# One order changed in the expert layer: how activations and gates come back from DRAM, which tile is picked first, how many dots stand beside U, and where the lower halves are made

## The reference

```
idx = i1[ci // 16] * 128 + i2[ci % 16];  g = softmax(sc)
act = gelu(sum_d u[idx, d] * h[d]) * g
out = sum_k act[k] * v[idx[k]]          # 8 heads x 16 experts = 128 picks a token
```

## Time and profile before

| what | us |
| --- | --- |
| median of 3 runs | 4067.66 (4053.11 to 4087.13) |
| the profiled execution's own time | 4076.54 |
| its span | 4075.3 |
| TensorE busy in the span | 3770.3 (93%) |
| VectorE busy | 2367.9 (58%) |
| ScalarE busy | 1348.4 (33%) |
| GpSimd busy | 552.5 (14%) |

### The profile page before, as it was taken

One profiled execution on the slowest core, in us unless ns is written; L12 is line 12 of the kernel. 1 busy time (PEld: TensorE's weight loads), 2 busy tenths in 40 slices (PEclk: granted clock), 3 DMA queues, 4 the chain that ended last, 5 costly groups with the idle time before them and its releaser, 6 DMA issues. The chain is left out here.

```text
span 4075.3 us, 46458 instructions
## 1 busy us (share of the span) xinstructions
PE 3770.3 (93%) x18298; PEld 3085.7 (76%) x18298; DVE 2367.9 (58%) x4034; ACT 1348.4 (33%) x2352; POOL 552.5 (14%) x612
## 2 busy tenths in 40 slices
PE   9889999999798999499999788999999999689999
PEld 7767999877776777378787667887888777467877
DVE  5746898877677888743337764332333266933332
ACT  3353333444233333232233334222322233333221
POOL 8500000011444444400000000000000000100000
PEclk9779999999899999799999879999999999789999
DMA  3003465688999999722222102222222221012222
GB/s 125 9 26 94 128 190 178 231 285 285 346 354 344 346 353 343 270 88 93 98 78 74 48 1 73 93 93 98 78 94 96 95 75 55 18 37 83 93 99 73
DMA packets 273433, 574.70 MB, mean 141 GB/s; under 512 B 19952, under 2 KB 159376, under 8 KB 271552
## 3 DMA queue, kind: packets, MB, share of 16 engines
q1 hardware_dynamic: 236256, 437.42, 32.4%
q0 software_dynamic: 36864, 134.23, 9.1%
q10 hardware_dynamic: 96, 0.08, 0.0%
HBM read 517.92 MB, written 53.74 MB: 140 GB/s over the span
## 5 line engine op out<-in xcount | busy, mean ns | idle before, releaser
L348 DVE TENSOR_TENSOR wlast<-wraw,wlast 128x1024 fp32r<-128x1024 f32 x406 | 495.2, 1225 | 506.4 <-ACT wlast L338 505.9
L357 PE MATMUL ps<-XH,wlast 128*128 128x512 f32 (+2 forms) x1888 | 734.0, 389 | 17.4 <-ACT arena L2020 17.4
L359 PE MATMUL ps<-XH,wlast 128*128 128x512 f32 (+2 forms) x1888 | 708.4, 375 | 0.0
L358 PE MATMUL ps<-XL,wlast 128*128 128x512 f32 (+2 forms) x1888 | 707.8, 375 | 0.0
L338 ACT ACTIVATE wlast<-wraw 128x1024 fp32r<-128x1024 f32 x406 | 424.8, 1051 | 246.9 <-PE ps L359 231.6
L348 DVE TENSOR_TENSOR wtwo<-wraw,wtwo 128x1024 fp32r<-128x1024 f32 x212 | 259.4, 1225 | 311.2 <-ACT wtwo L338 310.6
L357 PEld LDWEIGHTS ps<-XH,wlast 128*128 128x128 f32 x1888 | 358.3, 190 | 76.9 <-ACT arena L2020 18.1
L358 PEld LDWEIGHTS ps<-XL,wlast 128*128 128x128 f32 x1888 | 359.1, 190 | 53.5
L359 PEld LDWEIGHTS ps<-XH,wlast 128*128 128x128 f32 x1888 | 357.3, 189 | 55.1
L357 PE MATMUL ps<-XH,wtwo 128*128 128x512 f32 (+1 forms) x960 | 374.5, 390 | 0.0
L358 PE MATMUL ps<-XL,wtwo 128*128 128x512 f32 (+1 forms) x960 | 362.5, 378 | 0.0
(11 more groups left out here) (489 smaller groups left out, 7054.4 us busy)
## 6 DMA issues: line engine op xcount, KB each, us to landing
wraw<-in_ut SPq DMA_DIRECT2D x128, 512.0 KB, 4.1
wraw<-in_v SPq DMA_DIRECT2D x128, 512.0 KB, 7.1
wraw<-in_ffn_gate SPq DMA_DIRECT2D x88, 512.0 KB, 3.5
wraw<-in_ffn_up SPq DMA_DIRECT2D x88, 512.0 KB, 3.5
wraw<-in_ffn_down SPq DMA_DIRECT2D x88, 512.0 KB, 3.4
wraw<-in_w_in SPq DMA_DIRECT2D x58, 512.0 KB, 3.7
acts<-arena SPq DMA_DIRECT2D x128, 192.0 KB, 4.6
gates<-arena SPq DMA_DIRECT2D x12, 2048.0 KB, 10.2
```

Of the source, the lines that this page charges most:

```text
L348: ve.e.tensor_tensor(W.items[n][8], W.rawof(n), W.items[n][7], ALU.subtract).then_inc(*ve.up("wlo", n))
L357: mm(out, lh, rh, start=start, stop=False)
L358: mm(out, lh, rl, start=False, stop=False)
L359: return mm(out, ll, rh, start=False, stop=stop)
```

## The change

- The activations lie in DRAM as 64 pairs (128 partitions x 2 x 384), so that one load brings two turns (384 KB, runs of 3 KB). The stores write half a pair (runs of 1.5 KB). There are three pair buffers instead of six single ones.
- Gates come back for 8 turns at a time (1536 KB, runs of 1 KB) instead of 4 (768 KB, runs of 512 bytes). The DMAs have the same number of runs each.
- At the end of U, SyncE issues two gate loads and three pair loads, one each in items 135 to 139, after that item's weight load and store (`loads0` is 135).
- In the V stage both engines take the weight split and the activation in another order, and the lower half of the activation comes after the dots and rows of the turn.
- The planner orders the units anew: first all that the gathered tile needs, then the other tiles. Its costs and budgets differ a little, and a quota of 1.5 dots an item stands in place of the leftover time. In V, dots and rows are spread at an even pace over 124 turns.
- The arena of that level is larger, since one table (MK) no longer shares memory with the scores.

By the new arithmetic: index known at item 30 (before 44), `norm` at 80 (before 82), gates in items 83 to 130, 90 dots beside U (before 60). Of the 48 gate turns 28 have one dot and 20 have two. Items 131 to 143 have 20 dots, 1 or 2 each, and item 81 has two. V gets 38 dots and 128 rows, one or two a turn (four in two turns), and none is left behind turn 127.

```diff
@@ Peer.__init__
-        ar = k.level(12704)
+        ar = k.level(14752)
...
-        self.ad = k.nc.dram_tensor("acts", (128, 128, TOKENS), F).ap()
+        self.ad = k.nc.dram_tensor("acts", (64, 128, 2 * TOKENS), F).ap()
...
-        self.GC = [ar(4 * DENSE, 4, 32) for _ in range(2)]
-        self.AI = [ar(TOKENS) for _ in range(6)]
+        self.GC = [ar(4 * DENSE, 8, 32) for _ in range(2)]
+        self.AI = [ar(2, TOKENS) for _ in range(3)]
@@ schedule
+        first = [("top", c, GATHERED) for c in range(16)] + [("rows",)] + pick(GATHERED) + [("index",)]
+        tops = [("top", c, i) for c in range(16) for i in range(DENSE)]
+        rest = [u for i in range(DENSE) for u in pick(i)] + [("norm",), ("turned",)]
+        rest += [("gate", n) for n in range(self.GATES)]
...
-            time = min(time, 2.0) + (4.4 if kind == "wq" else 3.0)
+            time = min(time, 1.5) + (4.4 if kind == "wq" else 3.05)
+            quota = min(quota + self.RATE, 2.0) if known is not None and n >= known + 4 else 0.0
             while time > 0:
...
+                late = tops and first and first[0][0] == "top" and tops[0][1] <= first[0][1] - self.SCORES
+                if first and ready(n, first[0]) and not late:
+                    u = first.pop(0)
+                elif tops and ready(n, tops[0]):
+                    u = tops.pop(0)
+                elif not first and not tops and rest and ready(n, rest[0]):
+                    u = rest.pop(0)
+                elif quota >= 1 and dots < PICKS:
+                    u, quota, dots = ("dot", dots), quota - 1, dots + 1
+                else:
                     break
...
+        pace = (len(later) - 4) / 124
         for j in range(128):
-            time = min(time, 1.0) + 1.78
-            while later and time > 0:
+            quota += pace
+            while later and (quota >= 1 or later[0][0] == "act"):
@@ sp_u
+        ahead = [lambda: self.sp_gc(0), lambda: self.sp_back(0), lambda: self.sp_back(1), lambda: self.sp_gc(1),
+                 lambda: self.sp_back(2)]
...
-            if n == self.loads0:
-                for c in range(2):
-                    self.sp_gc(c)
-                for j in range(self.BACK):
-                    self.sp_back(j)
+            if n >= self.loads0 and ahead:
+                ahead.pop(0)()
@@ sp_act
-        sp.e.dma_start(self.ad[j], self.TT[j % 3]).then_inc(...)
+        half = slice(TOKENS * (j % 2), TOKENS * (j % 2) + TOKENS)
+        sp.e.dma_start(self.ad[j // 2, :, half], self.TT[j % 3]).then_inc(...)
@@ sp_gc, sp_back
-            sp.wait_ge(*at("ag", 4 * c - 5))
-        src = self.gd[:, :, 128 * c:128 * c + 128].rearrange("g p n -> p g n")
+            sp.wait_ge(*at("ag", 8 * c - 9))
+        src = self.gd[:, :, 256 * c:256 * c + 256].rearrange("g p n -> p g n")
...
+        if q >= 3:
+            sp.wait_ge(*at("al", 2 * q - 5))
+        sp.wait_ge(*at("astore", 2 * q))
+        sp.wait_ge(*at("astore", 2 * q + 1))
+        sp.e.dma_start(self.AI[q % 3].rearrange("p a t -> p (a t)"), self.ad[q]).then_inc(...)
@@ ve_prep, ve_low (new)
         v.tensor_tensor(x3, x3, self.GC[...], ALU.mult).then_inc(*ve.up("ag", j))
+
+    def ve_low(self, j):
         ve.wait_ge(*at("ah", j))
...
@@ ac_v
         for j in range(128):
-            split_ac(k, ("V", j))
             if j + self.LEAD < 128:
                 self.ac_prep(j + self.LEAD)
+            split_ac(k, ("V", j))
@@ ve_v
         for j in range(self.LEAD):
             self.ve_prep(j)
+            self.ve_low(j)
         for j in range(128):
-            split_ve(k, ("V", j))
             if j + self.LEAD < 128:
                 self.ve_prep(j + self.LEAD)
+            split_ve(k, ("V", j))
             for u in self.later[j]:
                 does[u[0]](*u[1:])
+            if j + self.LEAD < 128:
+                self.ve_low(j + self.LEAD)
@@ sp_v
-            if j >= 1 and j + self.BACK - 1 < 128:
-                self.sp_back(j + self.BACK - 1)
-            if j % 4 == 1 and (j - 1) // 4 + 2 < 32:
-                self.sp_gc((j - 1) // 4 + 2)
+            if j % 2 == 0 and j // 2 + 3 < 64:
+                self.sp_back(j // 2 + 3)
+            if j % 8 == 5 and j // 8 + 2 < 16:
+                self.sp_gc(j // 8 + 2)
```

More of the change, by code:

```diff
@@ L1873, in __init__, with pick @@
         self.schedule()
-    ROWS, SCORES, CHUNK = 5, 8, 32
+    ROWS, SCORES, CHUNK, RATE = 5, 8, 32, 1.5
     GATES = TOKENS // 8
     def schedule(self):
[L1882 to L1890, removed]
+        def pick(i):
+            return [("cand", i)] + [("best", i, h) for h in range(8)] + [("places", i)] + [
+                ("soft",)] * (i == 2) + [("mark", i, 0), ("mark", i, 1)]
+        cost = {"top": 1.7, "rows": 1.3, "cand": 2.5, "best": 2.3, "places": 2.5, "soft": 0.8, "mark": 7.0,
+                "index": 0.3, "norm": 2.1, "turned": 3.5, "gate": 2.7, "dot": 1.22}
+        first = [("top", c, GATHERED) for c in range(16)] + [("rows",)] + pick(GATHERED) + [("index",)]
+        tops = [("top", c, i) for c in range(16) for i in range(DENSE)]
+        rest = [u for i in range(DENSE) for u in pick(i)] + [("norm",), ("turned",)]
+        rest += [("gate", n) for n in range(self.GATES)]
         self.items = [("wq", c) for c in range(16)] + [("U", j) for j in range(128)]
@@ L1893, in schedule, with ready @@
         self.extras = [[] for _ in range(len(self.items) + 1)]
-        time, turn, known, dots = 0.0, None, None, 0
+        time, turn, known, dots, quota = 0.0, None, None, 0, 0.0
+        def ready(n, u):
+            return not (u[0] == "top" and n < u[1] + 2 or u[0] == "turned" and n < turn + 2
+                        or u[0] == "gate" and ("gate", u[1] - 1) in self.units[n])
         for n, (kind, c) in enumerate(self.items):
-            time = min(time, 2.0) + (4.4 if kind == "wq" else 3.0)
+            time = min(time, 1.5) + (4.4 if kind == "wq" else 3.05)
+            quota = min(quota + self.RATE, 2.0) if known is not None and n >= known + 4 else 0.0
             while time > 0:
[L1898 to L1902, removed]
+                late = tops and first and first[0][0] == "top" and tops[0][1] <= first[0][1] - self.SCORES
[8 more added lines that the diff above has]
+                else:
                     break
                 time -= cost[u[0]]
+                self.units[n].append(u)
                 if u[0] == "gate":
-                    time += 0.8
+                    time += 1.4
                     self.extras[n + 1].append(u)
@@ L1914, in schedule @@
                     known = n
[L1915 to L1922, removed]
+                if u[0] == "dot" and dots % self.CHUNK == 0:
+                    self.extras[n + 1].append(("gelu", dots // self.CHUNK - 1))
+        assert not first and not tops and not rest
         gates = [n for n, x in enumerate(self.extras) if any(u[0] in ("turn", "gate") for u in x)]
         self.loads0 = max(gates) + 4
-        assert self.loads0 < len(self.items) - 1, self.loads0
+        assert self.loads0 < len(self.items) - 4, self.loads0
         later = [("dot", x) for x in range(dots, PICKS)] + [("act", c) for c in range(PICKS // self.CHUNK)]
         later += [("row", x) for x in range(PICKS)]
-        self.later, self.gelus, time, gelu = [[] for _ in range(128)], [[] for _ in range(128)], 0.0, 0
+        pace = (len(later) - 4) / 124
+        self.later, self.gelus, quota, gelu = [[] for _ in range(128)], [[] for _ in range(128)], 0.0, 0
         for j in range(128):
-            time = min(time, 1.0) + 1.78
-            while later and time > 0:
+            quota += pace
+            while later and (quota >= 1 or later[0][0] == "act"):
                 u = later[0]
@@ L1936, in schedule @@
                     break
-                time -= 0.4 if u[0] == "act" else 1.28
+                quota -= u[0] != "act"
                 if u[0] == "dot" and u[1] % self.CHUNK == self.CHUNK - 1:
@@ L2098, in ve_top @@
                         self.IXu[:, i, c // 2, c % 2, :], self.TMP[:, 0:128])
-        last.then_inc(*ve.up(*(("topped", c) if i == 3 else ())))
+        last.then_inc(*ve.up(*(("topped", c) if i == DENSE - 1 else ())))
     def ve_cand(self, i):
@@ L2240, in sp_u @@
                         *sp.dma(f"gstore{g % 2}", "gstore", g))
[L2241 to L2249 removed]
+            if n >= self.loads0 and ahead:
+                ahead.pop(0)()
+        for issue in ahead:
+            issue()
         self.sp_act(127)
```

36 lines of the change are left out of this document (18 added, 18 removed).

## The result

The changed kernel takes 4107.16 us (median of 4 runs, 4106.02 to 4116.81); the kernel before took 4069.72 in the 4 runs beside it. The ratio is 1.0083, 95% interval 1.0052 to 1.0114: 0.8% or 34 us slower. Its profiled execution took 4116.81 us, its span is 4115.6. The forecast was 4103.

The account below looks back on a forecast made before the run. V was taken as bound by VectorE's program order, waits first, then work. +39.0 - 22 + 10 + 5.6 + 4 = +36.6, about -1 for the clock: +36 us, 4103 against the median 4067.66; range 4068 to 4145.

Parts of the forecast that it names:

- The order chain: V stage: VectorE's split waits 1.61 us a turn for ScalarE's weight upper half; turn 5.30 us, net +39.0 us.
- the ring: V turn's closed sequence: product, activation's upper half, weight's upper half, split, row, lower half, next product; 3.71 us plus rows.
- U's end: End of U: 22 us won by V's earlier first product, 10 us lost to the new loads; bounds 0 and 22.
- Dots and DMA beside the gates: Gate turns beside U: second dots delay gate operands, 5.6 us; DMA has more to move, 4 us.
- Picking first: Picking part of U: same units in another order, TensorE stays full, VectorE at 94%; no cost.
- Sum: Whole kernel: the terms together give +36.6 us, then about -1 for the clock, so +36.
- the clock: TensorE's clock at the tail, half in both kernels: about -1 us.
- Rival A: V, VectorE's wait before the split: the chain does not bind, DMA decides; -96 us, 3972; 8%.
- B: SyncE's queue, items 135 to 143, stays full; U's loss 34 us instead of 10; +60, 4128; 22%.
- C: U ends clean: no loss there and none beside the gates; +17 us, 4085; 12%.
- Rival D: V: TensorE's idle time drops its clock to 1.2 GHz, turn 7.7 us; +300 us, 4370; 3%.
- TensorE's idle time at V's end: End of V: no rows left over, so TensorE idles under 10 us, against 45.3 before.

Follow-up runs that it names:

- e1: The changed kernel with ScalarE's two steps in V back in the old order, weight's upper half before the activation's; 4002.19 us, ratio 0.9825 to the kernel before.
- e2: The kernel before with only the new order in V on both engines; 4174.35 us, ratio 1.0228 to the kernel before.
- e12: The changed kernel with gates loaded as in the kernel before (768 KB, 512-byte runs, four turns a tile); 4098.64 us, ratio 1.0063.
- e8: e1 with the second 1.5 MB gates load issued in V's second turn instead of near U's end; 4011.38 us, ratio 0.9837.
- e7: e1 with 66 dots beside U instead of 90, so 24 dots and their rows move to V; 4029.39 us, ratio 0.9886.
- e9: e1 with each 1536 KB gates load in two of 768 KB, issued four turns apart, still 1 KB runs; 3955.96 us, ratio 0.9722.
- e11: e6 with VectorE's order in V as before the change; 3985.98 us, ratio 0.9801 to the kernel before.
- e6: e1 with gates loaded as in the kernel before (768 KB, 512-byte runs, tiles of four turns); 3967.77 us, ratio 0.9738.

## Why the prediction was right, and where it was off

- **The order chain** (forecast: turn 5.30, wait 1.61, +39.0). Confirmed by e1, e2, e12. The turn is 5.19, the wait 1.54, the stretch from first product to addition +34.3. Link by link the ring is as it was put together from the earlier trace rows: product to split 1405.63 - 1403.54 = 2.09, and the eight turns with 11 rows from 1395.83 to 1438.62 take 42.79 where 8 x 3.71 + 11 x 1.20 = 42.9. The wait reads 1.54 and not 1.61 because the profile counts idle time from the product's end (0.55), not from when the next instruction could have started (0.48); no time hangs on that. The mean of 5.19 is lower than 5.30 since it counts the three first activations as turns; the 124 whole turns took 5.28. Most of what is left, 4.7 us of the sum, is the price of a dot. I had 1.22 for each of 38; from start to start it takes 1.15 (1096.92 to 1098.07 above), which is 2.8 us in all. The last split up to the addition took 1.1 us (1753.27 to 1754.40) where I had 2.2, and the rest is rounding.
- **U's end** (-22 + 10, bounds 0 and 22 on the loss). Joint -7.3, of it +1.4 beside the gates, so -8.7: a loss of 13 rather than 10. SyncE was hardly held (its gates' issues took 0.37 and 0.44 us where the earlier trace rows had 8.30, and the longest issue of a weight 2.67), but gelus still waited up to 8.27 us for stores. Its parts: 3.5 us are the deeper gates tiles (e12; e8 has 3.6), and the dots beside U's last items and gates together 9.1 (e7, 24 fewer).
- **Dots and DMA beside the gates** (5.6 + 4). Far too much. First to last gate matmul, over the same 48 gates, took 272.1 us before (746.1 to 1018.2) and 273.4 after (750.0 to 1023.4), +1.4 before rounding. TensorE waited for the gate operands 9.1 us in 47 waits before and 10.0 in 46 after: the operand that I had 0.31 us late in 20 turns must be made up elsewhere in the turn (where, I did not follow), and TensorE is busy 240.00 of 240 us. Two terms were also miscounted: 20 x 0.31 is 6.2, not 5.6, and 2% of 273 us is 5.5, not 4.
- **Picking first** (0). TensorE 260.00 of 260 us, VectorE 244.68 (94%), as forecast.
- **Sum**: forecast +36.6 less 1 for the clock, profile +27.0 up to TensorE's resumption and +0.9 behind it. Order and gates were 4.7 and 8.2 too high, U's end 3.3 too low; the median came near (4107 against 4103) partly by luck: the medians differ by 37 us, more than the 27 that the profiles account for.
- **Rival A** was the world of e1 and e9. Its condition was right (the chain gone, VectorE at 3.7 us and DMA to decide), and its 3972 lay between them: 4002 with the large loads, 3956 with half of them. 380 GB/s as a ceiling was too low, since e9 has 392 over 450 us. The Trainium skill (DMA: Bandwidth & Descriptors, Specifications) gives about 358 GB/s for one core's HBM limit, and the same page (Bandwidth) calls it what each core gets when both cores of a pair stream; this kernel runs on one core. e1's 355 looked like it, and e9's 392 at the same bytes a turn shows that it wasn't that limit. The measurement decides. The loss of nearer 20 us at U's end that the prediction drew from the figure does not come out of it: 4.33 MB at 358 GB/s are 12 us.
- **Rivals B, C.** V's first product came 623.0 us after the first gelu, where B (630.4 - 22 + 34) needs 642 and C (630.4 - 22) 608: neither.
- **Rival D.** The clock was 1.00 of 2.4 GHz over 1100 to 1700 us with TensorE busy 505.67 of 600 us, 84%, more than the 77% I had forecast. Lower readings (0.83, 0.60) stand only where TensorE had gaps of several us, at both joints. In e1 and e7, with gaps from late loads, they stand inside V as well (0.71 in e1's row above).
- **TensorE's idle time at V's end** was 6.22 us, under the 10 forecast.

## What to carry to other kernels

Before two engines' steps are swapped, draw the ring of who waits for whom within one turn: a step whose input was a turn old must not be queued behind one whose input is made in this turn. Here the swap on VectorE alone gains some 20 us where V is fed (e11 against e6), and the same swap on ScalarE costs 105 (after against e1). Judge a transfer by what is queued behind it, its landing time against the depth of the buffers it delays, before counting its bytes or the length of its runs; and a rate in a trace is what was asked for until another kernel with the same bytes shows that it can't be exceeded.

## What I had not expected of the hardware

DMA held 392 GB/s over 450 us in e9 (share 1.03), above the 380 of the best 20 us row before. The same bytes a turn moved at 355 GB/s with loads of 1536 KB in 1 KB runs, at 381 with 768 KB in 512-byte runs and at 392 with 768 KB in 1 KB runs. The last two differ in the depth of their tiles as well.
